# Prompt attention with six score buffers instead of four, and masked scores stored negated

## The reference

```python
def band_attention(q, k, v, q_pos, k_pos, k_valid, rel_bias):
    s = jnp.einsum('nqhd,nkhd->nhqk', q, k).astype(jnp.float32) * (HEAD_DIM ** -0.5)
    rel = jnp.clip(q_pos[:, None] - k_pos[None, :], -MAX_REL, MAX_REL) + MAX_REL
    s = s + rel_bias[:, rel].astype(jnp.float32)[None]
    s = jnp.where(k_valid[None, None, None, :], s, -1e30)
    p = jax.nn.softmax(s, axis=-1)
    return jnp.einsum('nhqk,nkhd->nqhd', p.astype(v.dtype), v)
...
    sh1, sc1, gt1, sh2, sc2, gt2 = ada_mod(c, w_ada, b_ada)
    h = rmsnorm(x, norm1_g) * (1 + sc1) + sh1
    q, k, v, cb, cc, cv, ga, gb = jnp.split(h @ w_in, IN_SPLITS, axis=-1)
...
    mix = (jax.nn.sigmoid(ga) * (att @ w_pa) + jax.nn.sigmoid(gb) * (conv_out @ w_pb)) @ w_o
    x = x + gt1 * mix
    h2 = (rmsnorm(x, norm2_g) * (1 + sc2) + sh2).reshape(n * L, D_MODEL)
    experts, weights = route(h2, w_group, b_group, w_expert, b_expert)
    ffn = moe_ffn(h2, experts, weights, w_e_gate, w_e_up, w_e_down).reshape(n, L, D_MODEL)
```

## Time and profile before

| | |
|---|---|
| median of 3 runs | 1816.34 us (1815.8 to 1818.95) |
| the profiled execution | 1819.63 us |
| its span, first to last instruction | 1818.0 us |
| PE busy | 1618.5 us (89% of the span) |
| VectorE busy | 957.5 us (53%) |
| ScalarE busy | 747.0 us (41%) |
| mean granted clock of TensorE | 0.959 of full speed |

### The profile page before, as it was taken

How to read it: one execution, slowest core, us unless ns; L and a number is a source line. 1 busy time by engine, 2 the same in 40 slices (tenths; PEclk the granted TensorE clock), 3 DMA queues, 4 the chain that set the end, 5 groups by cost and what they waited for, 6 DMA issues and landing times.

```text
span 1818.0 us, 22794 instructions
## 1 busy us (share of the span) xinstructions
PE 1618.5 (89%) x8729; PEld 1331.9 (73%) x8729; DVE 957.5 (53%) x1173; ACT 747.0 (41%) x869; POOL 230.1 (13%) x262
## 2 busy tenths in 40 slices
PE   6993999777899999999998995299999999999977
PEld 1243997445689899999997884278888888888853
DVE  0450110676511552222223555669888889888957
ACT  0221221565311031111212223068787777778763
POOL 2002600000000000000000001302112121212003
PEclk9996999899989999999999997599999999999989
DMA  9867711100831111111225333099999999999957
GB/s 342 274 126 165 265 58 53 44 1 1 311 90 35 48 35 53 48 53 55 81 60 198 117 115 116 25 386 395 399 388 405 386 400 393 398 392 398 393 214 291
DMA packets 145596, 364.04 MB, mean 200 GB/s; under 512 B 12491, under 2 KB 70899, under 8 KB 129010
## 3 DMA queue, kind: packets, MB, share of 16 engines
q1 hardware_dynamic: 121632, 289.92, 43.0%
q0 software_dynamic: 18976, 55.59, 9.8%
q10 hardware_dynamic: 4914, 17.49, 2.4%
HBM read 324.49 MB, written 47.89 MB: 205 GB/s over the span
## 4 chain that ended last, share of the span: by engine, by line
PE 75%; DVE 9%; DMA 8%; issue 3%; ACT 2%; another core or an unknown queue 2%; SPq 0%; DVEq 0%; POOL 0%; ACTq 0%; POOLq 0%; PEldq 0%
PE ps L1546 12%; PE ps L1547 12%; PE ps L1548 12%; DMA mraw<-in_w_e_down_dram 5%; PE ps L1867 5%; PE ps L1868 5%; PE ps L1874 5%; PE ps L1529 4%; PE ps L1894 2%; PE ps L1895 2%; PE ps L1902 2%; PE ps L1662 2%; PE ps L1672 2%; PE ps L1650 2%
## 5 line engine op out<-in xcount | busy, mean ns | idle before, releaser
L1059 DVE TENSOR_TENSOR mlo<-mraw,mhi 128x2048 fp32r<-128x2048 f32 x188 | 425.0, 2289 | 70.5 <-ACT mhi L926 70.1
L926 ACT CAST mhi<-mraw 128x2048 fp32r<-128x2048 f32 x192 | 360.7, 1915 | 104.5 <-DMA mraw<-in_w_e_down_dram 101.5
L1546 PE MATMUL ps<-hTh,ring_r 128*128 128x384 f32 x864 | 292.1, 338 | 38.1 <-DVE ring_r L1059 31.3
L1547 PE MATMUL ps<-hTl,ring_r 128*128 128x384 f32 x864 | 291.1, 337 | 0.0
L1548 PE MATMUL ps<-hTh,ring_r 128*128 128x384 f32 x864 | 290.8, 337 | 0.0
L1867 PE MATMUL ps<-mhi,xTh 128*128 128x512 f32 x512 | 204.1, 399 | 2.7 <-DVE xTl L1059 2.4
L1868 PE MATMUL ps<-mhi,xTl 128*128 128x512 f32 x512 | 201.1, 393 | 0.0
L1546 PEld LDWEIGHTS ps<-hTh,ring_r 128*128 128x128 f32 x864 | 163.9, 190 | 39.8 <-DVE ring_r L1059 29.5
L1059 DVE TENSOR_TENSOR ring_r<-ring_f,ring_r 128x1024 fp32r<-128x1024 f32 x56 | 68.3, 1224 | 199.6 <-ACT ring_r L732 199.3
L1547 PEld LDWEIGHTS ps<-hTl,ring_r 128*128 128x128 f32 x864 | 164.0, 190 | 0.0
L1548 PEld LDWEIGHTS ps<-hTh,ring_r 128*128 128x128 f32 x864 | 164.0, 190 | 0.0
(11 more groups left out here) (303 smaller groups left out, 2400.4 us busy)
## 6 DMA issues: line engine op xcount, KB each, us to landing
mraw<-in_w_e_gate_dram SPq DMA_DIRECT2D x64, 1024.0 KB
mraw<-in_w_e_up_dram SPq DMA_DIRECT2D x64, 1024.0 KB
mraw<-in_w_e_down_dram SPq DMA_DIRECT2D x64, 1024.0 KB, 11.7
aring<-in_w_ada_dram SPq DMA_DIRECT2D x24, 1024.0 KB
ring_f<-in_w_in_dram SPq DMA_DIRECT2D x80, 256.0 KB, 4.6
y_d<-yy ACTq DMA_DIRECT2D x32, 512.0 KB, 7.3
y_d<-zrow POOLq DMA_DIRECT2D x68, 128.0 KB, 4.1
kc<-in_cache_attn_k_dram SPq DMA_DIRECT2D x8, 1024.0 KB, 7.9
```

The lines of the kernel that those rows point to most:

```text
L926: nc.scalar.copy(mhi[j][:], mraw[j][:]).then_inc(s["gu_hi" if j < 4 else "d_hi"], 1)
L1059: V.tensor_tensor(out, value, high.bitcast(F32), ALU.subtract).then_inc(sig, 1)
L1546: mm(out, xh, wh, start=start, stop=False)
L1547: mm(out, xh, wl, start=False, stop=False)
```

## The change

Three edits. The masking operation multiplies by -1 and reduces with the minimum, so that what it writes is the negated score and what it reduces is directly the negated maximum; the exponential takes a factor of -1 and the multiplication that negated the maximum is dropped (64 in prompt attention, 8 in sample attention). S gets six buffers of 2.5 KB, from RING + 27 KB to RING + 42 KB, and `masked(a)` waits for the transposes of head a-6. PT stays where it was. Since S now begins inside the second key buffer, SP waits for the end of prompt attention before the keys of sequence 1, not behind them.

```diff
-        rowmax = small("rowmax", [P, 72])
...
-        S = at("S", [P, 4, BAND], X(0))
-        PT = [at(f"PT{j}", [P, 5, P], X(10 + 2.5 * j) if j < 2 else A(148.25)) for j in range(3)]
+        NS = 6
+        S = at("S", [P, NS, BAND], RING + 27 * KB)
+        PT = [at(f"PT{j}", [P, 5, P], RING + 42 * KB + 2560 * j if j < 2 else A(148.25)) for j in range(3)]
...
             def load_caches():
                 sp.wait_ge(s["unit_used"], NADA + UV + 4)
                 old_keys(0)
+                sp.wait_ge(s["s_attc"], HP * NPT)
                 old_keys(1)
                 sp.wait_ge(s["v_out"], 32)
-                sp.wait_ge(s["s_attc"], HP * NPT)
...
-                nc.scalar.activation(S[:, a % 4, c0:BAND], S[:, a % 4, c0:BAND], ACT.Exp,
+                nc.scalar.activation(S[:, a % NS, c0:BAND], S[:, a % NS, c0:BAND], ACT.Exp, scale=-1.0,
                                      bias=negmax[:, a:a + 1], accum_out=rowsum[:, a:a + 1]
                                      ).then_inc(s["s_p"], 1)
...
                 dve.wait_ge(s["s_scores"], a // 2 + 1)
-                wait(dve, s["s_pt"], a - 3)
-                link(V.tensor_tensor_reduce(out=S[:, a % 4, c0:BAND], in0=bank(2 * (a % 2), 2)[:, c0:BAND],
-                                            in1=bias[:, h, c0:BAND], scale=1.0, scalar=-3e38,
-                                            op0=ALU.add, op1=ALU.max, accum_out=rowmax[:, a:a + 1]))
-                V.tensor_scalar(negmax[:, a:a + 1], rowmax[:, a:a + 1], -1.0, None, ALU.mult
-                                ).then_inc(s["s_sb"], 1)
+                wait(dve, s["s_pt"], a - NS + 1)
+                V.tensor_tensor_reduce(out=S[:, a % NS, c0:BAND], in0=bank(2 * (a % 2), 2)[:, c0:BAND],
+                                       in1=bias[:, h, c0:BAND], scale=-1.0, scalar=3e38,
+                                       op0=ALU.add, op1=ALU.min, accum_out=negmax[:, a:a + 1]
+                                       ).then_inc(s["s_sb"], 1)
```

More of the change, by code:

```diff
@@ L832, in _ @@
                 wait(act, s["ks_pt"], q)
-                nc.scalar.activation(Ps[:], Ss[:], ACT.Exp, bias=negmax[:, 64 + q:65 + q],
+                nc.scalar.activation(Ps[:], Ss[:], ACT.Exp, scale=-1.0, bias=negmax[:, 64 + q:65 + q],
                                      accum_out=rowsum[:, 64 + q:65 + q]).then_inc(s["ks_p"], 1)
@@ L1114, in normed @@
                 link(V.reciprocal(rinv[:, a:a + 1], rowsum[:, a:a + 1]))
-                V.tensor_scalar(S[:, a % 4, c0:BAND], S[:, a % 4, c0:BAND], rinv[:, a:a + 1], None, ALU.mult
+                V.tensor_scalar(S[:, a % NS, c0:BAND], S[:, a % NS, c0:BAND], rinv[:, a:a + 1], None, ALU.mult
                                 ).then_inc(s["s_n"], 1)
@@ L1170, in _ @@
                 wait(dve, s["ks_p"], q)
[L1171 to L1175, removed]
+                V.tensor_tensor_reduce(out=Ss[:], in0=bank(4, 2)[:, 0:NK], in1=sbias[:], scale=-1.0,
+                                       scalar=3e38, op0=ALU.add, op1=ALU.min,
+                                       accum_out=negmax[:, 64 + q:65 + q]).then_inc(s["ks_sb"], 1)
                 if q >= 1:
@@ L1661, in prob_t @@
                 for j in range(4 - min(i, 4), 5):
-                    last = tr(bank(4, 2)[:, j * P:(j + 1) * P], S[:, a % 4, j * P:(j + 1) * P], ident[:])
+                    last = tr(bank(4, 2)[:, j * P:(j + 1) * P], S[:, a % NS, j * P:(j + 1) * P], ident[:])
                 last.then_inc(s["s_pt"], 1)
```

## The result

The changed kernel took 1795.86 us in the median (1789.0 to 1797.84, 4 runs), the kernel before 1817.64 beside it; the ratio of the two is 0.9871, with a 95% interval of 0.9839 to 0.9903. On the 1816.34 that the forecast started from, that is 1792.9 us, 23 us off. I had forecast 17, with a range that began at 1795: the direction was right, the size too small. It was not too small by much. In that comparison one execution of the kernel before took 5725 us and is left out.

A forecast was written before the change was run, and what follows sets the result against it. Prompt attention was taken as a loop of waits with no engine full. Saving 18 us there and paying 1 for late keys gave -17, from 1816.34 to 1799.3 us; range 1795 to 1809, the forecast's own 1796 to 1803.

The forecast's parts named there:

- the first head pair: Prompt attention's opening: six rounds of eight to gain in, part at the lower clock; saves 4.4 us (3.6 by long bound).
- the step from 19.6 down to 18: Prompt attention's saving was put at 19.6 or 15.8 us, and 18 was taken, nearer to the start-to-start distance.
- The negation: Prompt attention rounds: PE starts scores after the accumulator read, not the negation; 0.19 us less a round.
- The transposes leave the round: Prompt attention: with six buffers masking stops waiting for the second head's transposes; full round 5.21 to 4.47 us.
- short bound: Masking starts 0.24 us behind the column copy's start; 4.9 us saved a head pair, 19.6 in prompt attention.
- long one: Masking must see the column copy out, 0.36 us; 3.9 us saved a head pair, 15.8 in prompt attention.
- opening and tail: Start and end of prompt attention, outside the head pairs' terms: 0.5 us saved.
- The late keys: Sample attention: second key load waits for prompt attention's end; +1 us taken, between -1.5 and +2.9.
- The rival of the clock in sample attention: Clock falls while the sample stage waits for keys, 10 to 14 us, costing 5 to 6: 1805 us; chance 0.18.
- Not only the negation pays: Denies the rival that only the negation pays, another wait replacing prompt attention's buffer wait: 1811.2 us; chance 0.12.
- The minimum is not dearer: Denies the no-effect rival: masking with a minimum costs 0.3 us more a piece, about 1817 us; chance 0.04.
- The clock did not stay down: Denies the slower rival: low clock through all eight sample rounds costs 29 us, giving 1828 us; chance 0.04.

The follow-up runs named there:

- the first traces: First profiled execution each of the kernel before and the changed kernel, nothing else altered: prompt attention 146.28 and 122.32 us.
- dummies in both kernels: 13 dummy PE matmuls in the first rounds of prompt attention, added to the kernel before (ratio 0.9967) and to the changed kernel (0.9855).
- the trace with the copy moved: Changed kernel with the copy of the attention columns behind both maskings instead of between them: ratio 0.9829 to the kernel before.

## Why the prediction was wrong, point by point

The gain in prompt attention was put at 18 us and measured 24.0 in the first traces. Of the 6 us, 4.0 are the first head pair, 1.6 the step from 19.6 down to 18, and 0.4 the later head pairs. Another 0.9 lies in sample attention (+0.1 instead of +1), and 1.2 in stages that do not change (-0.7 and -0.5). At equal low clock prompt attention gained 20.3 to 20.7.

**The negation:** right. 0.19 a round, 1.52 a head pair alone; the minimum with factor -1 costs what the maximum did (median 752 ns over the 64 maskings against 754).

**The transposes leave the round:** right in mechanism. The column copy took their place and the masking follows it by 0.21 us, nearer the short bound (0.24) than the long one (0.36). The three later head pairs were forecast at -14.7 by the short bound, and -0.5 for opening and tail; they measured -5.28, -5.02 and -5.27 (the last with its tail), 15.6. Taking 18 instead of the 19.6 of the short bound, as a hedge, was the smaller part of the miss: 1.6 us.

**The first head pair:** this is the step that failed. I put 4.4 us on it; it gave 8.4 in the first traces and 8.3 in the second. At equal low clock it gives 32.12 - 27.24 = 4.9, and with dummies in both kernels 29.99 - 25.32 = 4.7, close to the 4.4. What I had left out is that its low stretch is not a fixed length. I had read it in the trace ("part of it ran at the lower clock level") and used it only to make the transposes dearer. The stretch was 10.2 us shorter in the changed kernel in both pairs of traces; at 0.3 to 0.4 us a microsecond that is the missing 3 to 4 us. Whether the change makes it shorter stays open. Six executions of versions with five or six buffers and the multiplication by -1 dropped (all without dummies) were at 0.50 in the first head pair for 0, 3.4, 3.4, 6.8, 6.8 and 10.2 us; five executions of four-buffer versions for 10.2, 10.2, 13.7, 13.7 and 17.1. But each part alone shows no shorter stretch: 17.1 us with the negation dropped, 13.7 with six buffers. The two together may be what it takes, or chance has a large share in so few executions.

**The late keys:** forecast +1, measured +0.1: 1.7 for the stage's opening, less 7 x 0.18 = 1.3 for its rounds (5.79 against 5.97) and 0.3 because the last round before ran into the low clock (6.27). The rounds gained in full, so the transfers don't bind here. They are not far from it: with the negation alone, which also has rounds of 5.79, one round waited 0.51 us for its new value rows and took 6.35. The Trainium skill's figure that I weighed there ("DMA: Bandwidth & Descriptors", section Bandwidth: near 358 GB/s) would give a round of 5.95, an estimate from the 2.13 MB of keys, values and new rows that it loads; the even part of the stage moved 372 GB/s (above), so the trace doesn't bear it out here.

**The rival of the clock in sample attention:** its sign came (the clock fell at 439 us; I had named 445), but not its price. In the first trace after, the keys were 1.07 us late and the clock fell:

```profile
433.58 5.45 DMA kc<-in_cache_attn_k_dram
439.03 0.04 issue
439.07 1.85 PE ps L1694 x8
440.93 0.85 PE ps L1718 x4
441.78 0.21 PE ps L1719
442.00 1.26 PE ps L1694 x8
443.25 1.01 PE ps L1729 x32
```

The transposes of keys took 1.85 where they take 0.9 at full clock, yet the first value matmuls came 9.57 us into the stage; in the second execution, with the clock at 1.00, they came at 9.82, held by the new value rows. Slow matmuls filled a wait that was there anyway. That the fall would last 10 us or more was wrong, it was 3.4. Costing nothing was luck of position. In the trace with the copy moved the same 3.4 us began behind the first value matmuls, the next score matmuls took 1.93 us instead of 1.06, and the round took 6.78 instead of 5.79.

**The other rivals** fell. Not only the negation pays: alone it gave 8.2 us in the total. The minimum is not dearer (752 ns against 754). The clock did not stay down: 0.93 over the sample stage, 1.00 in its even part.

**The range** had no room on the fast side. Every rival was slower than the forecast, and the lower end was the sum of the best bounds of the terms (-21.1, which is 1795.2 and not the 1796 given there). A stretch of low clock that could come out shorter was in no term and no rival.

## What to carry to other kernels

Before costing a buffer, write down the round: which link closes it, and which will close it next. The full rounds then came out within 0.1 us of their forecasts (4.42, 5.02, 4.61 and 3.92 us against 4.47, 5.02, 4.56 and 4.0), and the next link (a small copy in the wrong place of an engine's list) was worth about half of the change, 10.2 us of prompt attention. A term for a stretch at lower clock must allow for the stretch itself coming out longer or shorter, not only for what it does to the loop. And a hedge between two bounds is not information: where a row supports one of them, take it.

## What the runs showed of the hardware

A stretch at 0.50 in the opening of this loop, which is mostly waits, cost 0.3 to 0.4 us a microsecond (33.52 against 32.12 us for 3.4 us of it, 25.13 against 23.81 for 3.4, 27.24 against 25.12 for 6.8). A group of value matmuls, one behind the other, took 1.94 us at 0.50 against 1.03 at full clock, so a loop without waits would lose about half, an estimate from these two. The same program drew low stretches of 13.7 and 10.2 us in one place in two executions, and its sample stage ended at full clock or at 0.50 (2.8 or 4.0 us for the same instructions). Together that is 1.4 and 1.5 us between two executions of one kernel, so a difference of that size needs no other cause.

The masking of 128 x 640 scores took 0.81 to 0.82 us, plus 0.08 for the read of its accumulator, with the maximum and a factor of 1 and with the minimum and a factor of -1.
